# Values beside ones in one stationary matrix, the masks behind the next scores, the last down banks in the order of their next use, and two value rounds moved out of the attention

## The reference, cut to what matters

```python
def _fox_prompt(q, k, v, lf):            # swept in blocks of 128 queries
    ...
        s = jnp.einsum('bqhd,bkhd->bhqk', qi, k).astype(jnp.float32) * scale
        s = s + ci[..., None] - c_keys[:, :, None, :]
        mask = (pos[None, :] <= pi[:, None]) & (pos[None, :] >= pad)
        s = jnp.where(mask, s, NEG_INF)
        p = jax.nn.softmax(s, axis=-1).astype(v.dtype)
        return jnp.einsum('bhqk,bkhd->bqhd', p, v)
...
def _fox_sample(q, k, v, lf, ck, cv, clf, page_table):
    k_all = jnp.concatenate([ck[page_table].reshape(b, -1, h, dh), k.astype(ck.dtype)], axis=1)
    v_all = jnp.concatenate([cv[page_table].reshape(b, -1, h, dh), v.astype(cv.dtype)], axis=1)
    ...
    return jnp.einsum('bhqk,bkhd->bqhd', p, v_all)
...
def _ffn(x, w_gate, w_up, w_down, g, b):
    hdn = jax.nn.silu(x @ w_gate) * (x @ w_up)
    return _layer_norm(ALPHA * x + hdn @ w_down, g, b)
```

## Time and profile before

| | us |
|---|---|
| median of the runs | 1769.67 |
| lowest and highest of 3 runs | 1766.85, 1770.70 |
| the profiled execution's own time | 1766.5 |
| its span, first to last instruction | 1764.8 |
| PE busy | 1707.0 (97% of the span) |
| DVE, ACT, POOL busy | 803.0, 408.3, 751.0 |
| mean granted TensorE clock | 0.984 |

### The profile page before, as it was taken

How to read it: one execution, slowest core, us unless ns; L and a number is a source line. 1 busy time by engine, 2 the same in 40 slices (tenths; PEclk the granted TensorE clock), 3 DMA queues, 4 the chain that set the end, 5 groups by cost and what they waited for, 6 DMA issues and landing times.

```text
span 1764.8 us, 29361 instructions
## 1 busy us (share of the span) xinstructions
PE 1707.0 (97%) x11760; PEld 1561.5 (88%) x11760; DVE 803.0 (45%) x1282; ACT 408.3 (23%) x740; POOL 751.0 (43%) x584
## 2 busy tenths in 40 slices
PE   7999999998999899999999999999999999999995
PEld 7967677775888899999999999999999999999994
DVE  4156767541424251111274857534534533542527
ACT  4033333322224351111120642110110010011133
POOL 4310101100212203333354646886686686686325
PEclk9899999999999999999999999999999999999998
DMA  5244444413663021111112221111121121121202
GB/s 162 62 116 123 128 123 133 127 32 85 193 173 68 20 66 49 48 48 41 43 48 72 70 74 36 55 55 36 54 65 33 48 67 37 47 62 44 89 25 97
DMA packets 176012, 130.28 MB, mean 74 GB/s; under 512 B 22394, under 2 KB 148762, under 8 KB 175762
## 3 DMA queue, kind: packets, MB, share of 16 engines
q1 hardware_dynamic: 170258, 127.24, 24.9%
q10 hardware_dynamic: 5632, 1.35, 0.5%
HBM read 117.63 MB, written 10.92 MB: 73 GB/s over the span
## 4 chain that ended last, share of the span: by engine, by line
PE 86%; DVE 7%; ACT 2%; issue 2%; DMA 1%; SPq 1%; POOL 0%; DVEq 0%; ACTq 0%; POOLq 0%
PE psum L1646 7%; PE psum L1651 6%; PE psum L1650 6%; PE psum L1003 5%; PE psum L1007 5%; PE psum L1006 5%; PE psum L1064 4%; PE psum L1068 4%; PE psum L1070 4%; PE psum L1711 4%; PE psum L1713 4%; PE psum L1712 4%; PE psum L1219 3%; PE psum L1548 3%; PE psum L1552 3%; PE psum L1551 3%
## 5 line engine op out<-in xcount | busy, mean ns | idle before, releaser
L866 POOL CAST wh<-raw 128x1024 fp32r<-128x1024 f32 x72 | 87.5, 1215 | 772.3 <-PE psum L1064 383.8
L868 POOL TENSOR_TENSOR wl<-raw,wh 128x1024 fp32r<-128x1024 f32 x72 | 190.2, 2641 | 5.8
L896 POOL TENSOR_TENSOR wl<-raw,wh 128x512 fp32r<-128x512 f32 x126 | 168.7, 1339 | 10.1
L1064 PE MATMUL psum<-xh,wh 128*128 128x352 f32 (+1 forms) x480 | 162.3, 338 | 1.5 <-DVE ql L2419 1.5
L1646 PE MATMUL psum<-xh,wh 128*128 128x258 f32 x576 | 162.5, 282 | 0.0
L1650 PE MATMUL psum<-xl,wh 128*128 128x258 f32 x576 | 162.4, 282 | 0.0
L1651 PE MATMUL psum<-xh,wl 128*128 128x258 f32 x576 | 162.2, 282 | 0.0
L1068 PE MATMUL psum<-xl,wh 128*128 128x352 f32 (+1 forms) x480 | 160.7, 335 | 0.0
L1070 PE MATMUL psum<-xh,wl 128*128 128x352 f32 (+1 forms) x480 | 159.5, 332 | 0.0
L3013 DVE TENSOR_TENSOR mixed<-mixed,psum 128x344 f32<-128x344 f32 x216 | 108.4, 511 | 78.1 <-PE psum L1713 78.0
L1711 PE MATMUL psum<-hh,wh 128*128 128x344 f32 x432 | 139.2, 322 | 1.5
(11 more groups left out here) (396 smaller groups left out, 4351.5 us busy)
## 6 DMA issues: line engine op xcount, KB each, us to landing
raw<-in_w_in SPq DMA_DIRECT2D x86, 256.0 KB, 3.6
parts<-in_cache_k SPq DMA_DIRECT2D x64, 256.0 KB, 3.0
parts<-in_cache_v SPq DMA_DIRECT2D x64, 256.0 KB, 3.0
raw<-in_w_gate SPq DMA_DIRECT2D x44, 256.0 KB, 3.1
raw<-in_w_up SPq DMA_DIRECT2D x44, 256.0 KB, 2.9
raw<-in_w_down SPq DMA_DIRECT2D x44, 256.0 KB, 2.9
raw<-in_w_o SPq DMA_DIRECT2D x28, 256.0 KB, 3.1
cb<-negc_scratch SPq DMA_DIRECT2D x8, 520.0 KB, 5.1
```

The source lines that it names most:

```text
L1064: ins = mm(out, wt(wh, slot, k), xh[:, k, c0:c0 + cw], start=(k == 0), stop=False)
```

## The change

The slots of `vx` become three of 64 columns: the values of head 0, ones, the values of head 1. One stationary matrix of 128 columns, [values, ones] or [ones, values], gives a head's product and its row sums in one bank, so `mix` issues two matmuls where it issued four. `mix_copy` copies four halves of 64 partitions where it copied two of 128, the ones are set once by two memsets on DVE, and the values are stored by four DMAs a pair in place of two, in rows of 64 numbers. The tile's mask moves behind the main matmuls of `scores` (or behind `maxima_at`). The rounds of the samples: round 1 moves from step 15 to 17, rounds 2 and 3 go to the next stretch, whose rounds and `sample_outputs` are dealt out anew; `own(1)` goes behind `logits(0)` on DVE. In `down_new` the last six units take the banks in the order 6, 7, 2, 3, 4, 5, and `unit_done` is counted by the next matmul in place of PE's wait, except at the very last unit.

```diff
@@ -71,7 +71,7 @@
...
-DOWN_BANKS = [6, 7, 4, 5, 2, 3]
+DOWN_BANKS = 3 * [6, 7, 4, 5, 2, 3] + [6, 7, 2, 3, 4, 5]
...
@@ -205,14 +205,14 @@
...
-ROUNDS_AT = {14: 0, 15: 1, 16: 2, 17: 3}
+ROUNDS_AT = {14: 0, 17: 1}
...
-FRONT_PART = 11
+FRONT_PART = 7
...
@@ -389,8 +389,8 @@
...
-        vx = [a(f"vx{e}", [P, NT, P]) for e in range(2)]
-        of, rec = a("of", [P, 2, SEG]), a("rec", [P, SEG])
+        vx = [a(f"vx{e}", [P, NT, 3, DH]) for e in range(2)]
+        sums_of = a("sums_of", [P, SEG])
...
@@ -622,9 +622,11 @@
...
-                sp.dma_start(o[0:8 * P, P * j:P * j + P].rearrange("(t p) c -> p t c", p=P), v[:, 0:8, :])\
-                    .then_inc(sem("kv_stored"), 16)
-                sp.dma_start(o[8 * P:TP, P * j:P * j + P], v[0:TAIL, 8, :]).then_inc(sem("kv_stored"), 16)
+                for h in range(2):
+                    sp.dma_start(o[0:8 * P, P * j + DH * h:P * j + DH * h + DH].rearrange("(t p) c -> p t c", p=P),
+                                 v[:, 0:8, 2 * h, :]).then_inc(sem("kv_stored"), 16)
+                    sp.dma_start(o[8 * P:TP, P * j + DH * h:P * j + DH * h + DH], v[0:TAIL, 8, 2 * h, :])\
+                        .then_inc(sem("kv_stored"), 16)
...
@@ -660,8 +662,8 @@
...
             values_part(FRONT_PART)
-            for r in range(4, ROUNDS):
-                p = {4: 21, 6: 22, 9: 23, 12: 24}.get(r)
+            for r in range(2, ROUNDS):
+                p = {3: 21, 5: 22, 8: 23, 12: 24}.get(r)
                 if p is not None:
                     panel(p, column_of(p))
                 for c in range(2 * r + 4, min(2 * r + 6, PARTS)):
@@ -1131,6 +1133,18 @@
...
+            unmasked = [None]
+
+            def mask_tile():
+
+                if unmasked[0] is None:
+                    return
+                w, m = unmasked[0]
+                unmasked[0] = None
+                for b in ST_BANKS:
+                    last = mm(psum[0:w, b, 0:m], identb[0:w, 0:w], early[0:w, 0:m], start=False, stop=True)
+                last.then_inc(sem("tile_full"), 1)
...
             def scores(p, i, n, rows_before):
...
                     rows = slice(DH * h, DH * h + DH)
                     last = mm(psum[0:nq, b, 0:c1 - c0], qh[rows, i * P:i * P + nq], kh[rows, c0:c1],
                               start=True, stop=not diagonal)
+                mask_tile()
                 if diagonal:
                     for b in ITEM_BANKS:
                         last = mm(psum[0:nq, b, d0:d0 + nq], identb[0:nq, 0:nq], later[0:nq, 0:nq],
@@ -1195,11 +1210,9 @@
...
                 if diagonal:
-                    m = min(P, n)
-                    for b in ST_BANKS:
-                        last = mm(psum[0:w, b, 0:m], identb[0:w, 0:w], early[0:w, 0:m], start=False,
-                                  stop=True)
-                last.then_inc(sem("tile_full"), 1)
+                    unmasked[0] = (w, min(P, n))
+                else:
+                    last.then_inc(sem("tile_full"), 1)
...
@@ -1210,14 +1223,14 @@
...
                 if first and SEGS * j + s > 0:
-                    pe.wait_ge(sem("o_copied"), 2 * (SEGS * j + s))
+                    pe.wait_ge(sem("o_copied"), 4 * (SEGS * j + s))
                 pe.wait_ge(sem("probs_ready"), 2 * (g + 1))
-                for part, b in enumerate(MIX_BANKS):
-                    for h in range(2):
-                        cols = slice(DH * h, DH * h + DH)
-                        left = vx[j % 2][0:w, t, cols] if part == 0 else ones[0:w, cols]
-                        last = mm(psum[cols, b, off:off + n], left, pt[0:w, g % RING_P, h, 0:n], start=first,
-                                  stop=end)
+                if g == 0:
+                    pe.wait_ge(sem("consts_ready"), 3)
+                for h, b in enumerate(MIX_BANKS):
+                    left = vx[j % 2][0:w, t, h:h + 2, :].rearrange("p a d -> p (a d)")
+                    last = mm(psum[:, b, off:off + n], left,
+                              pt[0:w, g % RING_P, h, 0:n], start=first, stop=end)
                 last.then_inc(sem("mixed_in"), 1)
...
@@ -1315,6 +1328,7 @@
...
                 maxima_at(j, x, 0)
+                mask_tile()
                 if g >= 1:
                     mix(g - 1)
...
                     for u in SUMS_AT.get(x, ()):
...
-            sample_outputs(0)
             pe.wait_ge(sem("probs_ready"), 2 * STEPS * 4)
-            pe.wait_ge(sem("o_copied"), 2 * SEGS * 4)
+            pe.wait_ge(sem("o_copied"), 4 * SEGS * 4)
...
@@ -1343,44 +1356,47 @@
...
             G0 = PAN_GLA + GH
             whole(G0 - 1, 0, "gate")
+            sample_outputs(0)
+            value_round(2)
             gate_logits(0, FRONT["logits"])
             whole(G0 - 1, 1, "gate")
-            value_round(4)
+            value_round(3)
             sample_outputs(1)
             whole(G0 - 1, 2, "gate")
+            value_round(4)
+            whole(G0, 0, "q")
             value_round(5)
-            whole(G0, 0, "q")
-            value_round(6)
             sample_outputs(2)
             whole(G0, 1, "q")
+            value_round(6)
+            whole(G0, 2, "q")
             value_round(7)
-            whole(G0, 2, "q")
-            value_round(8)
             sample_outputs(3)
             whole(G0 + 1, 0, "k")
+            value_round(8)
+            whole(G0 + 1, 1, "k")
             value_round(9)
-            whole(G0 + 1, 1, "k")
-            value_round(10)
             sample_outputs(4)
             whole(G0 + 1, 2, "k")
+            value_round(10)
+            whole(G0 + 2, 0, "v0")
             value_round(11)
-            whole(G0 + 2, 0, "v0")
-            value_round(12)
             sample_outputs(5)
             whole(G0 + 2, 1, "v0")
+            value_round(12)
+            whole(G0 + 2, 2, "v0")
             value_round(13)
-            whole(G0 + 2, 2, "v0")
-            value_round(14)
             sample_outputs(6)
             for b in FRONT["k"]:
                 settled(b)
             turn((ke,), FRONT["kt"], [])
-            value_round(15)
+            value_round(14)
             for b in FRONT["v0"]:
                 settled(b)
             whole(G0 + 3, 0, "v1")
+            value_round(15)
+            whole(G0 + 3, 1, "v1")
             sample_outputs(7)
-            whole(G0 + 3, 1, "v1")
             whole(G0 + 3, 2, "v1")
...
@@ -1647,6 +1663,8 @@
...
+                        if n > 1 and (job_, v, c, k) == (0, S1, 0, 0):
+                            first.then_inc(sem("unit_done"), 1)
...
@@ -1696,7 +1714,7 @@
...
-                        b = DOWN_BANKS[x_ % 6]
+                        b = DOWN_BANKS[x_]
                         take(b)
...
@@ -1708,13 +1726,15 @@
...
-                            mm(out, w[0], x[0], start=(k == 0), stop=False)
+                            first = mm(out, w[0], x[0], start=(k == 0), stop=False)
+                            if (c, m, k) == (2, 4, 0):
+                                first.then_inc(sem("unit_done"), 1)
                             mm(out, w[1], x[0], start=False, stop=False)
                             last = mm(out, w[0], x[1], start=False, stop=(k == 1))
                             if c == 2 and m % 4 == 3 and k == 0:
                                 last.then_inc(sem("unit_done"), 1)
                         give(b, last)
-                        if c == 2 and m % 4 == 3:
+                        if (n, c, m) == (SEVENS, 2, 7):
                             pe.wait_ge(bank_full[b], B.before(b))
                             pe.sem_inc(sem("unit_done"), 1)
...
@@ -1888,12 +1908,14 @@
...
-                        read(b, do(v[:, 4 * g:4 * g + 4, :], bank(b).rearrange("p (t c) -> p t c", t=4), ACT.Copy))
+                        read(b, do(v[:, 4 * g:4 * g + 4, 0:3:2, :],
+                                   bank(b).rearrange("p (t h d) -> p t h d", t=4, h=2), ACT.Copy))
...
@@ -1931,7 +1953,10 @@
...
                 for h, b in enumerate(MIX_BANKS):
-                    do(of[:, h, 0:n], psum[:, b, 0:n], ACT.Copy).then_inc(sem("o_copied"), 1)
+                    mine, other = slice(DH * h, DH * h + DH), slice(DH * (1 - h), DH * (1 - h) + DH)
+                    do(o32[mine, j, SEG * s:SEG * s + n], psum[mine, b, 0:n], ACT.Copy)\
+                        .then_inc(sem("o_copied"), 1)
+                    do(sums_of[mine, 0:n], psum[other, b, 0:n], ACT.Copy).then_inc(sem("o_copied"), 1)
...
@@ -2396,6 +2421,9 @@
...
             filled(3)
+            dve.wait_ge(sem("negc_ready"), 1)
+            for e in range(2):
+                ve.memset(vx[e][:, :, 1, :], 1.0).then_inc(sem("consts_ready"), 1)
             ve.tensor_copy(slf[:, :], psum[0:NB, 3, NT * FH:(NT + 1) * FH]).then_inc(sem("slf_ready"), 1)
...
@@ -2474,9 +2502,10 @@
...
-                dve.wait_ge(sem("o_copied"), 2 * (SEGS * j + s + 1))
-                link(ve.reciprocal(rec[:, 0:n], of[:, 1, 0:n]))
-                ve.tensor_tensor(o32[:, j, SEG * s:SEG * s + n], of[:, 0, 0:n], rec[:, 0:n], ALU.mult)\
```

(19 more changed lines are left out.)

## The result

The changed kernel takes 1756.7 us (median of nine runs, 1752.15 to 1761.08) against 1767.2 us of the kernel before: a ratio of 0.994, 95% interval 0.9927 to 0.9954, 10.5 us less where 20.9 less were forecast. The profiled execution took 1754.67 us with a span of 1752.9, 11.9 us less than the span before.

The account below looks back on a forecast made before the run. PE was taken to set the pace, with DVE not far behind. Attention -14, seam +1.8, feed-forward -9.3 and start +0.6 sum to -20.9 us, from the median of 1769.7 to 1748.8, forecast as 1749; range 1739 to 1757.

Parts of the forecast that it names:

- feed-forward term: Feed-forward rounds: PE's waits at unit m = 4 (0.31 us, nine times) and S1 (0.81, eight times) vanish, -9.3 us.
- the attention: All attention steps: mix and masks gain 22 us, 8 are lost again, -14 us.
- Mix, -17: Attention steps: two full-width matmuls for four half-width ones save 14.6 us in 56 long steps, 2.4 in 16 short.
- the rival worked out beside it: Mix: halves already run side by side, so merging gives nothing; sum -7.9 us, 1762 us, chance 0.14.
- sign of that drain: First projection matmul behind L1219: 0.27 us to the next start instead of 0.16, read as draining at a mode change.
- Masks, -5: Diagonal attention steps: masks beside full-width matmuls save one entry and exit, about 0.2 us in 25 steps, 5 us.
- Lost to DVE, SP and ACT, +8: First three pairs: SP's longer queue costs 4 us, ACT's four copies 1.6, the third pair 0.8, new waits 1.6.
- 512 B: Stores of values: with 256-byte rows, below the skill's 512 B, they would land later and raise the sum; no size given.
- Seam, +1.8: End of attention into feed-forward: -10.9 + 3.0 - 2.6 + 5.2 + 2.6 + 4.5 us, bounds -1 and +6.
- Start, +0.6: Kernel start: two memsets on DVE take 1.05 us against 0.48 idle, so PE's next chunk is 0.6 us later.
- The rivals: Merging gives nothing, 1762 us, 0.14; attention becomes DVE's, 1759, 0.18; S1 waits for something else, 1755, 0.07; slower, 1799, 0.04.
- The attention becomes DVE's: Attention: DVE sets the pace, only the last pair's 5.5 us and some 2 more stay; 1759 us, chance 0.18.

Follow-up runs that it names:

- e8: The changed kernel with the next query chunk's copy put between the first two and last two of ACT's four copies behind a pair's first segment: 1752.6 us, 0.9908.
- e5: The changed kernel with sample_outputs(1) to (6) each one chunk and one round later: 1744.3 us, 0.9864 of the kernel before.
- e10: e5 with the wait for the last four copies moved from ahead of the first gate chunk to behind it: 1741.3 us, 0.985.
- e9: e5 with no part of the cached keys in steps 4 to 6 of a pair, the parts spread over other steps: 1752.4 us, 0.9921.
- e1: The kernel before with only the feed-forward part (order of the last six down banks, unit_done counted by the next matmul): 1757.9 us, 0.9949.
- e4: The kernel before with only the value rounds moved and own(1) put behind the logits: 1769.4 us, 1.0016.
- e3: The kernel before with only the merged mix, its ones, copies, stores and memsets: 1766.9 us, 0.9999.
- e7: The changed kernel with a pair's four stores of values issued ten steps later on SP, behind the query's spread: 1753.5 us, 0.9924.
- e6: The changed kernel with 30 matmuls that nobody reads filling PE's wait ahead of sample_outputs(1): 1753.3 us, 0.9907.

## Why the prediction was half right

The sign, the range and the feed-forward term held; the point was 8 us too low, and the attention is the step that failed: -7.4 us for -14.

That the time lies inside the forecast's own range, 0.3 us below its upper end of 1757, is luck in part. The range was laid from 1769.7 us, so it stood for -31 to -13 us; beside the changed kernel the kernel before took 1767.2, and the measured -10.5 is outside. Most of that gain is the feed-forward part; of the attention's only half came.

**Mix, -17.** The mechanism was right, the size was not: -12.8. "That is 0.26 us less" for 272 queries measured 0.20. The new records cost what was forecast: the four start at 335.38, 335.67, 335.90 and 336.13 us, so 0.23 us each from the second on, but the first takes 0.29, and these 0.06 us were left out. Of the 16 short steps, the eight of 128 queries won the 0.15 each that were forecast; those of 16 and 144 lost.

What was won is a border, not columns. A step of 384 queries took 284.90 - 283.19 = 1.71 us before and takes 285.79 - 284.28 = 1.51 now:

```profile
283.19 0.87 PE L1219 MATMUL psum<-pt,vx 128*64 128x384 f32 x4
...
284.90 0.32 PE L1064 MATMUL psum<-xh,wh 128*128 128x344 f32 x1
```

```profile
284.28 1.51 PE L1232 MATMUL psum<-pt,vx 128*128 128x384 f32 x4
...
285.79 0.32 PE L1066 MATMUL psum<-xh,wh 128*128 128x344 f32 x1
```

That is 0.20 us again, and 112 more columns cost 0.38 us in both kernels: column for column, eight half-width records run as fast as four of full width. So the rows agree with up to twice the rate of the Trainium skill, TensorEngine Tiling (Array Packing), Theoretical Speedup, but not with the rival worked out beside it, that nothing is left to gain. Key Properties of the same page, draining at a change of mode, goes with the border ahead of the mix that shrinks, by 0.1 us, only where the matmul ahead fills the array. The forecast's own sign of that drain does not hold: it took the 0.27 us from the first projection behind L1219 to the next start for it, but behind the full-width mix, with no change of mode, the same interval is 336.51 - 336.16 = 0.35 us.

**Masks, -5.** About 4 in the undisturbed steps; -3.0 as a time.

**Lost to DVE, SP and ACT, +8.** About 8.6, an estimate: the third pair won 4.3 us, and the first two together kept nothing. So the size held; the shortfall of the attention is in the mix (4.2 us), the masks (1) and the last steps that the table counts with the seam. Both causes are where the forecast put them. These are ACT's four copies, with the query copy behind them:

```profile
113.58 0.47 ACT L1957 ACTIVATE o<-psum 64x384 f32<-64x384 f32 x1
114.08 0.49 ACT L1959 ACTIVATE sums_of<-psum 64x384 f32<-64x384 f32 x1
114.59 0.49 ACT L1957 ACTIVATE o<-psum 64x384 f32<-64x384 f32 x1
115.10 0.48 ACT L1959 ACTIVATE sums_of<-psum 64x384 f32<-64x384 f32 x1
115.61 0.46 ACT L1889 ACTIVATE qh<-psum 128x352 fp32r<-128x352 f32 x1
```

From the start of the first copy to that of the query copy it is 2.03 us, where it was 1.04: 1.0 us more, for the forecast's 0.8. e8 takes back the 1.0 us of PE's wait that this costs. On SP the four stores of the second pair and the spread behind them:

```profile
187.05 1.18 SPq L626 DMA_DIRECT2D out_v_prompt<-vx  x1
188.26 0.67 SPq L628 DMA_DIRECT2D out_v_prompt<-vx  x1
188.97 0.44 SPq L626 DMA_DIRECT2D out_v_prompt<-vx  x1
189.45 0.78 SPq L628 DMA_DIRECT2D out_v_prompt<-vx  x1
...
199.50 0.42 SPq L608 DMA_DIRECT2D qb<-sq_scratch  x1
```

3.1 us against 2.0, so 1.1 us more and not 2.0; yet the spread was issued 2.3 us later than before, and DVE's wait of 2.16 us became 3.7. What the term lacked was the clock behind PE's two longest waits, an estimated 1.2 us each: in the step behind each of them PE falls another 0.9 us back, where it should have won 0.3. The 512 B that the Trainium skill, DMA: Bandwidth & Descriptors, Specifications, asks for did not show as a late landing: the median store of 256 KB in rows of 256 B landed in 3.1 us, the 512 KB in rows of 512 B before in 4.5. The sizes differ, so no run here measures what the short rows cost.

**Seam, +1.8.** +4.2, inside its bounds of -1 to +6. From step 14 to the first gate chunk it is 10.6 us less, for 10.9; the 5.1 us (the forecast's terms give 5.1, not the 5.2 that it wrote) and the five waits (0.81 for 0.9) came out as worked out. Two sizes did not: the clock also fell behind the 1.77 us ahead of the first chunk (5.4 us for 4.0), which the forecast had only in its upper bound, and behind the 5.1 us it cost 3.5 for 2.6. e5 shows that the waits for `own_v` came from the order of the sums, e10 that the 1.77 us and the slow chunk behind them came from the wait for the copies.

**Feed-forward, -9.3.** -10.9 in the profile (1.30 us in each of eight rounds, 0.4 in the last), -8.9 as a time. The borders themselves gave the 0.31 and 0.81 us; the matmul behind each also comes 0.07 us sooner, against the rows above, which the forecast had not counted.

**Start, +0.6.** 0.8: PE's wait there is 2.29 us where it was 1.47. The other 1.4 us arise before 26 us, where nothing was changed; PE's first wait for split weights (4.0 us here, 3.5 before) lies between 3.3 and 4.0 us in the kernels here.

**The rivals.** None happened as told. "The attention becomes DVE's" came nearest: its attention term of -7.5 is what the profile shows (-7.4), and its time of 1759 lies 2 us from the measured one, the forecast's 8. It was true of steps 4 to 7 in two pairs, by way of late inputs; but it let only the last pair keep its gain, and the third kept it too. In the first pair an earlier query copy (e8) and fewer parts of the keys (e9) each took the long wait down, so lateness and DVE's work are not apart there.

Outside the seam every term of the forecast was in time at full clock. As a cross-check, time x mean clock has a median of 1740 us before (the 29 runs beside e1 to e4) and 1721 after, 19 us apart, close to the 20.9; the mean clock fell from 0.985 to 0.979. That product counts all slow time as work, so 10 us is the most that the clock can have taken, and which stalls trigger it in the median run, no profile here says.

## What to carry to other kernels

Where PE is 97% busy, a term won on PE is kept only as far as every input of the next waits comes earlier too. So follow the queues that feed DVE before adding up PE's gain, and reckon with a stretch at half clock behind a new PE wait of a few microseconds: here it came behind four of them and not behind others. When a consumer is moved next to its producer, look at the engine between them: here moving six lines back gained as much again as the whole change.

## What was not expected of the hardware

The same stall is not always followed by the slow clock. PE waits 2.96 us for `qe` in the profile before and 2.95 in that of e3, ahead of the same matmul; before, the clock stayed at 1.00 from 588 to 594 us, in e3 it fell:

```profile
591.67 0.40 PE L1398 MATMUL psum<-xh,wh 128*128 128x344 f32 x1 [2.96 <-DVE qe L2633]
```

```profile
587.50 0.40 PE L1400 MATMUL psum<-xh,wh 128*128 128x344 f32 x1 [2.95 <-DVE qe L2644]
```

```profile
588.00:590.00 2.00, 2.00 (x9) 0.50 0.00 0
```

Over the runs of a kernel, time and mean clock go together (correlation -0.93 for the nine of the changed kernel), so much of the scatter of some 10 us is in the clock. The single traces show how much can lie in one stretch: from 530 to 660 us, where all kernels here have the same code, the mean clock is between 0.91 (e8) and 0.99 (e7), and 0.08 of 130 us are 10 us. That is why edits worth 1 to 3 us could be seen in profiles and not in times.

A DVE operation on two SBUF operands can stand still behind GpSimd. In e9 a product that takes 0.56 us elsewhere took 2.75, and ended 0.4 us behind POOL's split that had begun with it (DVE, then POOL):

```profile
147.11 2.75 DVE L2509 TENSOR_TENSOR o<-o,sums_of 128x384 f32<-128x384 f32 x1
```

```profile
147.09 2.35 POOL L871 TENSOR_TENSOR wl<-raw,wh 128x1024 fp32r<-128x1024 f32 x1
```

Such a collision delayed a `kl` for which PE then waited 2.4 us, once each in e6 and e7 (at 152 us) and twice in e9, and not in the other profiles. The Trainium skill, SBUF — State Buffer, SBUF: two separate sides, describes a port pair that DVE and GpSimd hold in turn for a whole instruction; these rows agree.
